# Modulation products of a two-block transformer kernel: column-tile panels replaced by whole-row chunks with quarter products

## The chip, the cores and the metric

One core of a Trainium2 chip runs the whole program in one launch. The metric is the device time in microseconds (us) of one execution; before the change three runs gave 1325.57, 1325.74 and 1326.34 us. The engines are named as in the profile: PE (TensorE matmul), PEld (its weight loads), DVE (VectorE), ACT (ScalarE), POOL (GpSimd) and SP (SyncE, which only issues DMAs here).

## The reference, cut to what matters

Two blocks of two layers each run on 256 tokens of width 1024. The first block is attention, a gated feed-forward and a per-layer embedding, twice. The second block modulates its inputs with vectors made from two conditioning vectors, `c` and `c_ctx`:

```python
mod_x = (silu_c @ w_mod[i] + b_mod[i])[:, None, :]       # silu_c: (1, 1024), w_mod[i]: (1024, 3072)
mod_c = silu_cc @ w_mod[i] + b_mod[i]
sh_x, sc_x, g_x = jnp.split(mod_x, 3, axis=-1)
hx = rms_norm_2(x, norm_g[i]) * (1.0 + sc_x) + sh_x
```

The change touches only the products `silu_c @ w_mod[i]` and `silu_cc @ w_mod[i]`: 1024 rows by 6144 columns over both layers, 25.2 MB of weights, for two vectors. They don't depend on the first block, so the kernel makes them beside it. The first 2048 columns (shift and scale of layer 0) are made during the first attention, 2048 more during each of the two feed-forwards.

## The kernel before, in words

Everything is float32. A large product `x @ w` is made of three fp32r products on PE (lines 417 to 419, `mm3`): high half by high half, high by low, low by high. The weights come as 295 panels of 128 x 1024 (512 KB each). SP loads them into six slots RAW, ACT copies each to its high half WH (line 1848), DVE subtracts to get the low half WL (line 1131), PE uses the pair. Three WH/WL slots turn over. Semaphores alone keep the engines in step; within an engine the order is that of the program text.

**First attention** (`attention("l0", ...)`, line 625). Sixteen units n = 0 to 15, two for each of 8 heads (even n one key block, odd n two). In PE's step n come, in this order: the scores of unit n (line 742), then `fill`, then for odd units the value product of unit n-3 (line 750, in the even steps from 4), then the transposes of unit n-2 (line 651). DVE adds the bias (1359), takes the maximum (1212) and later scales (1187, 1191, 1193). ACT in step n copies the transposes of unit n-2 (1887), makes the exponentials of unit n (1898), and in odd steps from n = 5 copies head (n-5)/2 out of PSUM (1997, `out_l0`), which lets POOL square that head (2523, `head_squares`). After the last unit come two groups of heads: POOL's squares, DVE's sum (1364), ACT's root (2007), DVE's reciprocal (1371) and product (1375), PE's transposes (759, `heads_turn`), ACT's and DVE's halves XH (2013) and XL (1384). Then the output projection `l0_o` begins (line 417, tile G).

**Fillers of the first attention.** `fill` (line 547) makes one 128-column product at a time: stationary the 32 padded vectors SC of k tile k, moving 128 columns of a panel of `w_mod`, plain float32. A panel holds one column tile of 128 columns with its eight k tiles. There are 16 panels and 128 such products: 12 before the attention, 5 in each of its steps 0 to 17, then 14, 6 and 6 around `heads_turn`. Each goes to a strip of 32 partitions of the PSUM bank O; four panels in a row use the same strip. The panels are loaded by POOL's queue (`panels`, line 2494, DMA at 2499) into six slots; before each `head_squares(h)` POOL issues panels up to `6 + (10*h + 35) // 8`: 4 to 9 ahead of the first head, 10 after the first head, and so on.

**Feed-forwards** (`ffn(layer)`). Tiles j = 0 to 21. In a tile PE makes `hidden` (48 matmuls into G, 128 columns of each of two halves), then `down` of the tile two before (24 into A). DVE scales and convolves, ACT and POOL (2473, 2474, 2477: HID, HH, HL) make the gated value that `down` uses. From tile 6 on each tile ends with a `refill` (line 571): a panel of 1024 columns of `w_mod` (two k tiles by 512 columns), which POOL loaded (`gathers`, 2501, DMA at 2509), ACT rounded to fp32r (2081, `high`) and DVE subtracted (1524, `rest`), takes four fp32r products of 512 columns into partitions 0 to 31 of O (line 578). SCR holds the vectors with their low halves (1453 to 1456). Four refills fill 512 output columns; ACT then copies the row to YR. Tiles 19, 20 and 21 and the last two `down` are written out after the loop.

**After each feed-forward**, in `ple`, ACT copies the last row (2139), PE turns the rows to columns (`turn_gathered`, 587), and DVE later adds the parts and the bias (`gathered`, 1413, 1404).

Of the kernel before, what the change touches and what calls it, by code (L numbers as in the profile page):

```python
# [23 lines left out]
P = 128  # L24
# [13 lines left out]
MODS = 48  # L38
PLAIN = 16
GROUPS = 4  # L40
# [95 lines left out]
def program(nc, x_tok, wst, wmod, vec, cst, x_t, ctx_t, p_t, pos, pos4, tab, rpb, lam4, grow, y_t):  # L136
    with ExitStack() as ctx:
# [31 lines left out]
        SCR = sb("SCR", [P, KD, 32], F32R)  # L169
# [51 lines left out]
        RM = mv[:, 6144:12288].rearrange("p (s c) -> p s c", s=RMS)  # L221
# [43 lines left out]
        YR = B[0:32, 2048:4608]  # L265
        RR = RM[:, 0:4, :]
        RH = XH[:, 12:16, :].rearrange("p n t -> p (n t)")
        RL = XL[:, 12:16, :].rearrange("p n t -> p (n t)")
        ROWS = HRS[:, 1, 0:32].rearrange("p (r t) -> p r t", r=2)
# [61 lines left out]
        r_raw = [sem(f"r_raw{i}") for i in range(4)]  # L331
        r_hi, r_lo, r_y = sem("r_hi"), sem("r_lo"), sem("r_y")
# [76 lines left out]
        def _(pe):  # L409
# [154 lines left out]
            def turn_modulators(dst):  # L564

                pe.wait_ge(m_y, 1)
                for q in range(4):
                    m = nc.tensor.transpose(dst[:, q * P:(q + 1) * P], YS[:, q * P:(q + 1) * P], IDT)
                m.then_inc(m_tr, 1)

            def refill(layer, s, i):

                if s == 0:
                    pe.wait_ge(r_y, i + (2 + 5 * layer))
                pe.wait_ge(r_lo, i * 4 + (5 + PLAIN * layer + s))
                for c in range(2):
                    for w in (RH, RL):
                        m = mm(O[0:32, :], SCR[:, 2 * s + c, :], w[:, 512 * c:512 * c + 512],  # L578
                               start=(s == 0 and c == 0 and w is RH), stop=(s == 3 and c == 1 and w is RL),
                               skip_group_check=True)  # L580
                m.then_inc(m_used, 1)

            def turn_gathered(layer):

                pe.wait_ge(r_y, 1 + 5 * (layer + 1))
                for t in range(PLAIN):
                    m = nc.tensor.transpose(O[:, 32 * t:32 * t + 32], YR[:, 512 + t * P:512 + (t + 1) * P], IDT[0:32, 0:32])
                m.then_inc(m_tr, 1)
# [36 lines left out]
            def attention(s, scores, value, filler=0, behind=None, meanwhile=(0, 0), first=0, last=None, ready=()):  # L625
                units = attn_units(s)
                width = 1 if s == "l0" else 2
                for n in range(first, len(units) + 3 if last is None else last):
# [7 lines left out]
                    if n < len(units) + 2:  # L636
                        fill(filler)
# [138 lines left out]
            turn_modulators(A[0])  # L776

            def ffn(layer):
# [37 lines left out]
                def tile(j, i=0, filled=None):  # L816
# [4 lines left out]
                    if filled is not None:  # L821
                        refill(layer, filled, i)

# [1912 lines left out]
```

## Time and profile before

| what | us |
|---|---|
| three timed runs, median | 1325.74 |
| three timed runs, lowest and highest | 1325.57, 1326.34 |
| span of the profiled execution, first to last instruction | 1325.0 |
| PE busy in it | 1271.4 (96%) |
| DVE busy | 945.7 (71%) |
| ACT busy | 723.9 (55%) |
| POOL busy | 391.0 (30%) |

The span is that of one other execution, and the table gives no time of its own for it beyond the span; the timed runs are 0.7 us longer than the span at their median, which is what lies around the first and last instruction. The records of a matmul overlap: its time on the chain is the distance to the next start, not its length. A plain float32 product of this program leaves two records, an fp32r product or a transpose one.

### The profile page before, as it was taken

What the parts mean: (1) busy time and instruction counts of PE and PEld (TensorE: products, weight loads), DVE (VectorE), ACT (ScalarE), POOL (GpSimd) and SP (SyncE); (2) the same over time, 40 slices, a digit from 0 to 9 for tenths busy, and PEclk for the clock granted to TensorE, in tenths of its full rate; (3) what the DMA queues carried; (4) which work ended last, traced back from release to release, by engine and by line L of the source; (5) the groups of instructions that cost most, each with busy time, mean ns of one, the idle gap of its engine ahead of it and who ended that gap; (6) DMA issues with size and microseconds to landing.
All of it is one profiled execution on the core that took longest, in us unless ns stands there. A gap on an engine that the chain in (4) does not pass through costs nothing.

```text
span 1325.0 us, 24391 instructions
## 1 busy us (share of the span) xinstructions
PE 1271.4 (96%) x8908; PEld 1102.8 (83%) x8908; DVE 945.7 (71%) x1426; ACT 723.9 (55%) x1257; POOL 391.0 (30%) x377
## 2 busy tenths in 40 slices
PE   5999999999999999999999999999989999999996
PEld 4887899999999877898999998888855699987666
DVE  6878588888878985558988887853377548454674
ACT  5555455655567777545565657644366515413562
POOL 4942144545431140143445452011012320000022
PEclk9999999999999999999999999999999999999999
DMA  8565246666645542155576663322200274522100
GB/s 309 178 218 191 72 141 233 219 222 219 217 154 172 160 130 96 63 191 171 197 234 211 230 213 128 130 93 95 96 1 1 59 181 133 170 95 80 48 1 32
DMA packets 52665, 191.72 MB, mean 145 GB/s; under 512 B 6048, under 2 KB 6304, under 8 KB 52320
## 3 DMA queue, kind: packets, MB, share of 16 engines
q1 hardware_dynamic: 43488, 158.59, 36.2%
q0 software_dynamic: 8368, 31.33, 7.5%
q8 instruction: 62, 1.02, 0.3%
q10 hardware_dynamic: 720, 0.57, 0.2%
q14 instruction: 27, 0.22, 0.0%
HBM read 189.41 MB, written 1.05 MB: 144 GB/s over the span
## 4 chain that ended last, share of the span: by engine, by line
PE 78%; DVE 9%; ACT 7%; issue 3%; POOL 1%; DMA 1%; SPq 0%; DVEq 0%; ACTq 0%; POOLq 0%
PE G L417 13%; PE G L419 13%; PE G L418 13%; PE A L417 6%; PE A L419 6%; PE A L418 6%; DVE WL L1131 3%; PE R L651 3%; PE R L578 2%; PE R L558 2%; ACT WH L1848 2%; PE A L999 1%; PE R L417 1%; PE R L419 1%; PE R L418 1%
## 5 line engine op out<-in xcount | busy, mean ns | idle before, releaser
L1131 DVE TENSOR_TENSOR WL<-RAW,WH 128x1024 fp32r<-128x1024 f32 x295 | 390.4, 1330 | 245.3 <-ACT WH L1848 244.9
L1848 ACT ACTIVATE WH<-RAW 128x1024 fp32r<-128x1024 f32 x295 | 310.4, 1057 | 387.1 <-PE G L419 275.9
L417 PE MATMUL G<-XH,WH 128*128 128x256 f32 (+1 forms) x1336 | 398.7, 298 | 7.8 <-DVE WL L1131 4.6
L419 PE MATMUL G<-XH,WL 128*128 128x256 f32 (+1 forms) x1336 | 395.4, 296 | 0.0
L418 PE MATMUL G<-XL,WH 128*128 128x256 f32 (+1 forms) x1336 | 395.4, 296 | 0.0
L417 PEld LDWEIGHTS G<-XH,WH 128*128 128x128 f32 x1336 | 255.5, 191 | 21.6 <-issue 10.6
L418 PEld LDWEIGHTS G<-XL,WH 128*128 128x128 f32 x1336 | 255.6, 191 | 7.4
L419 PEld LDWEIGHTS G<-XH,WL 128*128 128x128 f32 x1336 | 255.7, 191 | 6.2
L417 PE MATMUL A<-HH,WH 128*128 128x256 f32 x352 | 99.9, 284 | 1.0 <-POOL HL L2477 1.0
L418 PE MATMUL A<-HL,WH 128*128 128x256 f32 x352 | 99.8, 283 | 0.0
L419 PE MATMUL A<-HH,WL 128*128 128x256 f32 x352 | 99.7, 283 | 0.0
L2453 POOL CAST XH<-HRS 128x256 fp32r<-128x256 f32 x24 | 11.4, 474 | 267.3 <-DVE HRS L1745 267.3
L1212 DVE TENSOR_REDUCE SM<-A 128x2 f32<-128x1024 f32 (+1 forms) x80 | 67.7, 849 | 17.9 <-PE A L999 12.8
L417 PEld LDWEIGHTS A<-HH,WH 128*128 128x128 f32 x352 | 67.6, 192 | 2.2 <-ACT WH L1848 1.9
L1887 ACT ACTIVATE ATT<-R 128x1024 f32<-128x1024 f32 (+3 forms) x56 | 37.7, 674 | 56.8 <-PE R L651 56.8
L418 PEld LDWEIGHTS A<-HL,WH 128*128 128x128 f32 x352 | 67.6, 192 | 0.1
L419 PEld LDWEIGHTS A<-HH,WL 128*128 128x128 f32 x352 | 67.6, 192 | 0.0
L417 PE MATMUL G<-WH,XH 128*128 128x512 f32 (+1 forms) x136 | 54.6, 402 | 12.8 <-DVE XL L1157 11.1
L2473 POOL TENSOR_TENSOR HRS<-ATT,HRS 128x256 f32<-128x256 f32 x22 | 32.0, 1452 | 110.3 <-ACT HRS L2058 104.7
L2473 POOL TENSOR_TENSOR HRS<-HSQ,HRS 128x256 f32<-128x256 f32 x22 | 31.7, 1439 | 98.0 <-ACT HRS L2058 98.0
L417 PE MATMUL A<-WH,XH 128*128 128x512 f32 x144 | 57.4, 398 | 1.5 <-DVE XL L1469 1.3
L419 PE MATMUL A<-WH,XL 128*128 128x512 f32 x144 | 56.2, 390 | 0.0
(355 smaller groups left out, 2532.0 us busy)
## 6 DMA issues: line engine op xcount, KB each, us to landing
RAW<-in_wst SPq DMA_DIRECT2D x295, 512.0 KB, 4.1
M<-in_wmod POOLq DMA_DIRECT2D x48, 512.0 KB, 4.1
B<-in_rpb POOLq DMA_DIRECT2D x4, 1024.0 KB, 12.6
H<-in_x_t SPq DMA_DIRECT2D x2, 512.0 KB, 8.4
M<-in_x_tok SPq DMA_DIRECT2D x1, 1024.0 KB, 13.5
M<-in_ctx_t POOLq DMA_DIRECT2D x1, 1024.0 KB, 5.2
out_y<-M SPq DMA_DIRECT2D x2, 384.0 KB, 2.7
C<-in_cst SPq DMA_DIRECT2D x1, 737.0 KB, 15.1
```

Of the source, the lines that this page charges most:

```text
L417: mm(out, lh, rh, start=start, stop=False, skip_group_check=True)
L418: mm(out, lh, rl, start=False, stop=False, skip_group_check=True)
L419: return mm(out, ll, rh, start=False, stop=stop, skip_group_check=True)
L558: m = mm(out[32 * g:32 * g + 32, q * P:(q + 1) * P], SC[:, k, :], RM[:, i % RMS, k * P:(k + 1) * P], start=(k == 0), stop=(k == KD - 1), s ...
L578: m = mm(O[0:32, :], SCR[:, 2 * s + c, :], w[:, 512 * c:512 * c + 512], start=(s == 0 and c == 0 and w is RH), stop=(s == 3 and c == 1 and ...
L651: m = nc.tensor.transpose(ST[c][:, k * P:(k + 1) * P], PRB[a % 3][:, c, k * P:(k + 1) * P], IDT)
L999: m = mm(out[c][:, 0:nk * P], Q2[64 * c:64 * c + 64, t, qt * P:(qt + 1) * P], K2[64 * c:64 * c + 64, t // 4, k0:512], start=True, stop=Tru ...
L1131: v.tensor_tensor(WL[:, slot, :], RAW[:, raw, :], WH[:, slot, :].bitcast(F32), ALU.subtract).then_inc(w_lo, 1)
L1212: v.tensor_reduce(small(80, a, 2), sc, AX, ALU.max, negate=True).then_inc(at_mx, 1)
L1848: act(WH[:, slot, :], RAW[:, raw, :], ACT.Copy).then_inc(w_hi, 1)
L1887: act(att(s, j)[:, 0:width, 0:nk, q * P:(q + 1) * P], RO[:, :].rearrange("p (l k q) -> p l k q", l=2, k=4)[:, 0:width, 0:nk, :], ACT.Copy) ...
L2473: g.tensor_tensor(HID[b], CB[b][:, 0, :], SG[b], ALU.mult).then_inc(f_hid, 1)
```

## The change: what it does

The weights of the modulation are laid out anew on the host: 24 chunks of 128 x 2048 (1 MB each), one for each k tile and third of the 6144 columns. Everything is plain float32 now; a chunk is made of four products of 512 columns, one for each strip of 32 partitions of O ("quarter products"). In the first attention a chunk is taken in halves, with its two quarter products in one step: two halves ahead of the attention, one in each of the steps 1 to 14, none later. In each feed-forward eight chunks are used whole, one for every second tile, and ACT's and DVE's rounding, the row copies and the low halves SCR go. POOL copies the vectors of the chunk's k tile to SV before it issues each load. The output of a third is one bank O of 128 x 512, which ACT copies to YS and PE turns with four transposes.

```diff
+            def modulate(vectors, buf, start, stop):
+                for g in range(4):
+                    m = mm(O[32 * g:32 * g + 32, :], vectors, RM[:, buf, g, :], start=start, stop=stop, skip_group_check=True)
+                m.then_inc(m_used, 1)
+
             def fill(n):
                 for _ in range(n):
-                    i, k = divmod(fills[0], KD)
-                    if fills[0] == 0:
+                    i = fills[0]
+                    k, half = divmod(i, 2)
+                    if i == 0:
                         pe.wait_ge(m_sil, 1)
-                    if k == 0:
-                        pe.wait_ge(m_raw[i % RMS], 16 * (i // RMS + 1))
-                    g, q = i // 4, i % 4
-                    out = O
-                    m = mm(out[32 * g:32 * g + 32, q * P:(q + 1) * P], SC[:, k, :], RM[:, i % RMS, k * P:(k + 1) * P],
-                           start=(k == 0), stop=(k == KD - 1), skip_group_check=True)
-                    if k == KD - 1:
-                        m.then_inc(m_used, 1)
+                    pe.wait_ge(m_raw[i % RMS], 16 * (i // RMS + 1))
+                    for g in range(2):
+                        r = 32 * (2 * half + g)
+                        m = mm(O[r:r + 32, :], SC[:, k, :], RN[:, i % RMS, 512 * g:512 * g + 512],
+                               start=(k == 0), stop=(k == CHUNKS - 1), skip_group_check=True)
+                    m.then_inc(m_used, 1)
                     fills[0] += 1
...
-                    if n < len(units) + 2:
-                        fill(filler)
+                    if n in filler:
+                        fill(1)
...
-            fill(12)
+            fill(2)
             pe.wait_ge(bias_ok, 1)
-            attention("l0", scores_l0, value_l0, 5)
-            fill(14)
+            attention("l0", scores_l0, value_l0, range(1, 15))
             heads_turn(0)
-            fill(6)
             heads_turn(1)
-            fill(6)
...
                 for j in range(2, 7):
                     tile(j)
+                modulated(0, 0, start=True)
                 with pe.Fori(0, 3) as i:
-                    for d in range(4):
-                        tile(7 + d, i, d)
-                for d in range(3):
-                    tile(19 + d)
-                    refill(layer, d, 3)
+                    tile(7, i)
+                    tile(8, i)
+                    modulated(1, i)
+                    tile(9, i)
+                    tile(10, i)
+                    modulated(0, i + 1)
+                tile(19)
+                tile(20)
+                modulated(1, 3, stop=True)
+                tile(21)
                 down(0, p0 + 64, hb + FT - 1, p0 + 64, False, False)
-                refill(layer, 3, 3)
                 down(1, p0 + 65, hb + FT, p0 + 65, False, True)
...
-                        turn_gathered(layer)
+                        turn_modulators(O, 2 + layer)
...
-                        rest(d, i)
...
-                        high(d, i)
...
-                ac.wait_ge(m_used, PLAIN * (layer + 2))
-                act(YR[:, 2048:2560], O[0:32, :], ACT.Copy).then_inc(r_y, 1)
+                ac.wait_ge(m_used, PLAIN + CHUNKS * (layer + 1))
+                act(YS, O, ACT.Copy).then_inc(m_y, 1)
...
             def panels(first, end):
                 for i in range(first, end):
                     if i >= RMS:
                         gp.wait_ge(m_used, i - RMS + 1)
-                    gp.dma_start(RM[:, i % RMS, :], wmod[i]).then_inc(m_raw[i % RMS], 16)
+                    gp.dma_start(RN[:, i % RMS, :], wmod[i // 2][:, PW * (i % 2):PW * (i % 2) + PW]).then_inc(m_raw[i % RMS], 16)
...
+                g.tensor_copy(SV[:, k % 2, :], vectors).then_inc(r_vec[k % 2], 1)
+                src = wmod[first + k] if k < 2 else wmod[bass.ds(i * 2 + (first + k), 1)].rearrange("a p c -> p (a c)")
+                gp.dma_start(RM[:, k % 2, :, :].rearrange("p g c -> p (g c)"), src).then_inc(r_raw[k % 2], 16)
...
             for h in range(8):
-                upto = min(PLAIN, 6 + (10 * h + 35) // 8)
+                upto = min(PLAIN, 8 + 2 * h)
                 panels(nextp, upto)
                 nextp = upto
                 head_squares(h)
```

## Rows read from the trace of the kernel before

**Rows 1.** The page's busy times: us, share of the span, instructions
```profile
PE 1271.4 (96%) x8908; PEld 1102.8 (83%) x8908; DVE 945.7 (71%) x1426; ACT 723.9 (55%) x1257; POOL 391.0 (30%) x377
```
**Rows 2.** Busy by stretch: us, PE, PEld, DVE, ACT, POOL, PEclk, DMA share, GB/s
```profile
205.80:214.40 8.60, 8.60 (x74) 8.60 (x73) 6.32 (x10) 4.59 (x6) 3.91 (x3) 1.00 0.71 248
240.35:249.89 9.54, 9.54 (x78) 9.13 (x76) 8.18 (x11) 5.43 (x7) 4.50 (x4) 1.00 0.70 241
```
**Rows 3.** Timeline of PE: the starts of two feed-forward tiles without a refill
```profile
205.79 0.28 PE L417 MATMUL G<-XH,WH 128*128 128x256 f32 x1
...
214.44 0.28 PE L417 MATMUL G<-XH,WH 128*128 128x256 f32 x1
```
**Rows 4.** Chain in the first feed-forward: start us, us, what; two refills in a row
```profile
240.52 0.92 PE R L578 x4
...
250.06 0.92 PE R L578 x4
```
**Rows 5.** Timeline of PE, attention of the second block: two column strips of 64
```profile
970.70 1.95 PE L1008 MATMUL G<-ATT,M 128*64 128x256 f32 x16
972.58 1.13 PE L999 MATMUL A<-M 64*128 64x512 f32 x4
```
**Rows 6.** Timeline of the last tile of the first feed-forward
```profile
376.46 1.73 DVE L1524 TENSOR_TENSOR XL<-M,XH 128x1024 fp32r<-128x1024 f32 x1
377.07 1.73 POOL L2474 TENSOR_TENSOR HH<-HSQ,HRS 128x256 fp32r<-128x256 f32 x1
378.94 0.74 POOL L2477 TENSOR_TENSOR HL<-HRS,HH 128x256 fp32r<-128x256 f32 x1
...
379.83 0.36 PE L417 MATMUL A<-HH,WH 128*128 128x256 f32 x1 [0.48 <-POOL HL L2477]
```
**Rows 7.** Timeline of POOL in a tile without `rest`
```profile
217.57 0.75 POOL L2474 TENSOR_TENSOR HH<-ATT,HRS 128x256 fp32r<-128x256 f32 x1
```
**Rows 8.** Timeline of attention step 5, from the transposes to the next load
```profile
110.84 0.44 PE L651 MATMUL R<-C,ATP 128*128 128x128 f32 x2
...
112.49 0.39 ACT L1997 ACTIVATE B<-G 128x256 f32<-128x256 f32 x1
...
112.97 0.61 POOL L2523 TENSOR_TENSOR HRS<-B 128x256 f32<-128x256 f32 x1 [6.05 <-ACT B L1997]
...
113.53 0.59 POOL L2499 DMA_DIRECT2D M<-in_wmod  x1
```
**Rows 9.** Loads of `w_mod`, issued in 98.9:99.3 and in 113.4:114, to landing
```profile
DMA to landing us min/median/max: 6.0/6.0/6.0
DMA to landing us min/median/max: 3.9/3.9/3.9
```
**Rows 10.** Chain in the first attention: the fillers of steps 6 and 14
```profile
111.70 1.21 PE R L558 x10
...
130.54 1.21 PE R L558 x10
```
**Rows 11.** Timeline from the last sum of squares to the output projection
```profile
142.03 1.22 DVE L1364 TENSOR_REDUCE SM<-HRS 128x8 f32<-128x1024 f32 x1 [0.50 <-POOL HRS L2523]
...
144.26 1.26 ACT L2013 ACTIVATE XH<-A,SM 128x512 fp32r<-128x512 f32 x2 [3.44 <-PE A L759]
...
145.42 0.30 ACT L2007 ACTIVATE SM<-SM 128x8 f32<-128x8 f32 x1
...
145.99 1.29 DVE L1375 TENSOR_TENSOR B<-B,SM 128x512 f32<-128x512 f32 x2
...
147.20 2.72 DVE L1384 SCALAR_TENSOR_TENSOR XL<-A,SM,XH 128x512 fp32r<-128x512 f32 x4
...
149.35 0.39 PE L417 MATMUL G<-XH,WH 128*128 128x256 f32 x1
```
**Rows 12.** Timeline of PE: matmuls at the start, and one at 24 us
```profile
12.09 0.63 PE L419 MATMUL G<-WH,XL 128*128 128x512 f32 x1
...
24.30 0.39 PE L419 MATMUL G<-WH,XL 128*128 128x512 f32 x1
```

More of the change, by code:

```diff
@@ L168, in program @@
         SC = sb("SC", [P, KD, 32])
-        SCR = sb("SCR", [P, KD, 32], F32R)
+        SV = sb("SV", [P, 2, 32])
         mv = M[:, :]
@@ L330, in program @@
         sum_step = sem("sum_step")
-        r_raw = [sem(f"r_raw{i}") for i in range(4)]
-        r_hi, r_lo, r_y = sem("r_hi"), sem("r_lo"), sem("r_y")
+        r_raw = [sem(f"r_raw{i}") for i in range(2)]
+        r_vec = [sem(f"r_vec{i}") for i in range(2)]
         h_sq = sem("h_sq")
@@ L567, in turn_modulators @@
                 for q in range(4):
                     m = nc.tensor.transpose(dst[:, q * P:(q + 1) * P], YS[:, q * P:(q + 1) * P], IDT)
[L569 to L587, printed above, removed]
                 m.then_inc(m_tr, 1)
@@ L623, in advance, with attention @@
                     next(unit, None)
-            def attention(s, scores, value, filler=0, behind=None, meanwhile=(0, 0), first=0, last=None, ready=()):
+            def attention(s, scores, value, filler=(), behind=None, meanwhile=(0, 0), first=0, last=None, ready=()):
                 units = attn_units(s)
@@ L815, in ffn, with tile @@
                 hidden(1, p0 + 2, (u0 + 1) % 2, (u0 + 1) // 2, p0 + 2)
-                def tile(j, i=0, filled=None):
+                def tile(j, i=0):
                     q = p0 + 4 + 3 * (j - 2)
@@ L909, in _ @@
                                 + [(1, k) for k in range(8, 16)], T, lambda k: pe.wait_ge(at_g, AJ0["l1"] + k // 2 + 1))
-            attention("l1", scores_l1, value_l1, 0, first_o, (4, 3), first=2, ready=((1, TVALS),))
+            attention("l1", scores_l1, value_l1, (), first_o, (4, 3), first=2, ready=((1, TVALS),))
             advance(first_o, 32)
@@ L1025, in _ @@
             evacuated(pe, U0["a_z"] + 7)
-            attention("a", scores_a, value_a, 0, first_o, (2, 2), first=4)
+            attention("a", scores_a, value_a, (), first_o, (2, 2), first=4)
             advance(first_o, KD)
@@ L1099, in _ @@
             first_o = head_unit("b_o", [(c, k) for c in range(2) for k in range(7)] + [(0, 7), (1, 7)], T, lambda k: pe.wait_ge(at_o, AT_JOBS["a"] + k + 1))
-            attention("b", scores_b, value_b, 0, first_o, (6, 3), first=2, ready=((0, TVALS + 10), (1, TVALS + 12)))
+            attention("b", scores_b, value_b, (), first_o, (6, 3), first=2, ready=((0, TVALS + 10), (1, TVALS + 12)))
             advance(first_o, 2 * KD)
@@ L1397, in with_bias @@
             def with_bias(layer, r, t0, rows):
-                n = rows.shape[-1] if len(rows.shape) == 2 else rows.shape[-1] * rows.shape[-2]
+                n = rows.shape[-1] * rows.shape[-2]
                 at = VC[f"bm{layer}"] + t0
-                dst, bias = MD[:, layer, r, t0:t0 + n], V[:, at:at + n]
-                if len(rows.shape) == 3:
-                    dst, bias = (x.rearrange("p (g q) -> p g q", q=4) for x in (dst, bias))
+                dst, bias = (x.rearrange("p (g q) -> p g q", q=4) for x in (MD[:, layer, r, t0:t0 + n], V[:, at:at + n]))
                 link(v.tensor_tensor(dst, rows, bias, ALU.add))
@@ L1409, in scales, with modulators @@
                                             bc(V[:, VC[f"ng{layer}"]:VC[f"ng{layer}"] + 8], 2), ALU.add, ALU.mult))
[L1411 to L1424 removed]
+            def modulators(made, src, parts):
+                dv.wait_ge(m_tr, made)
+                rows = src.rearrange("p (q g r) -> p r g q", q=4, g=4)
                 for layer, t0, a, b in parts:
                     for r in range(2):
[L1427 to L1430 removed]
+                        with_bias(layer, r, t0, rows[:, r, a:b, :])
+                if made != 2:
+                    scales(made // 2)
+                v.memset(SM[:, 34 + made:35 + made], 0.0).then_inc(m_ok, 1)
             def add_out(tag, per, gain, late):
@@ L2075, in lands @@
                     return [16 * ((p + 3 + d) // RAWS + 1) for d in range(3)]
-                def high(s, i):
-                    ac.wait_ge(r_raw[s], i * 16 + (64 * layer + 16))
-                    ac.wait_ge(m_used, i * 4 + (PLAIN * (layer + 1) + s))
-                    act(RH, RR[:, s, :], ACT.Copy).then_inc(r_hi, 1)
-                def row(i, used):
-                    ac.wait_ge(m_used, used)
-                    act(YR[:, bass.ds(i * 512, 512)], O[0:32, :], ACT.Copy).then_inc(r_y, 1)
                 for j in range(2, 6):
```

76 lines of the change are left out of this document (23 added, 53 removed).

## The prediction

> **What bounds the kernel now.** I read the busy times first, then the chain of waits, then the timeline where the change cuts in. PE is busy for 96% of the span and the next engine for 71% [rows 1], so time is won by taking work from PE, where PE is the engine that nobody has to wait for. The feed-forwards are such a place. A tile without a refill takes 214.44 - 205.79 = 8.65 us [rows 3], a tile with one 250.06 - 240.52 = 9.54 us [rows 4]: the refill's 0.9 us lie bare on the path. In both kinds PE is busy to the last hundredth, while DVE has 6.3 of 8.6 and 8.2 of 9.5 us of work, ACT and POOL less [rows 2]. So the refill's PE time counts in full, and DVE's `rest` and ACT's `high`, which the change also takes out, count for nothing inside the tiles. The first attention is another kind of place: PE, DVE, ACT and POOL hand each unit on, and a pair of steps takes (130.54 - 111.70) / 4 = 4.71 us, of which the two fillers are 2 x 1.21 us [rows 10]. There the order in which POOL issues the loads matters, and that order is changed too.
>
> **Price of a quarter product.** Ten filler records of 128 columns take 1.21 us [rows 10], about 0.11 us each and 0.1 us for going in and out of the narrow strip. A pass over 512 columns is then 4 x 0.107 = 0.43 us, and a plain float32 product has two. Four strips one after the other would be 8 x 0.43 = 3.4 us. But the value products at line 1008, which go in turn to two strips of 64, put 16 passes of 256 columns, 3.4 us if done singly, into 972.58 - 970.70 = 1.88 us [rows 5]: two strips stream at once, at a cost of 0.15 us over half the single time. A half chunk of the attention has two strips: 0.86 + 0.15 = 1.0 us. No row shows four strips. The upper bound is 3.5 us a chunk (none side by side), the next 1.7 + 0.15 = 1.85 us (two by two), the lower 0.86 us (all four with nothing for the change of shape). I take 1.0 us, all four and the 0.15 us, since the nearest row shows different strips of one bank running wholly side by side.
>
> The Trainium skill speaks to this on two pages. *TensorEngine Tiling (Array Packing)*, "Tiling Modes", gives 128 x 32 as four tiles that work independently, and says that a change of mode drains the array; the 0.15 us in [rows 5] agree with the drain. *TensorE: Matmul & The Clock Gate*, "Why this matters for your kernels", reports only 2.38 times for three strips. An estimate by that page, 2.38 / 3 of four, is 3.4 / 3.17 = 1.08 us a chunk, and the sum below would be 1.3 us higher, 1324.5 us.
>
> **Feed-forwards.** In each one 14 refills stand before the last `hidden` ends; they go: 14 x 0.90 = 12.6 us. The last two stand behind it, where PE waits for the gated value of the last tile anyway (its `down` starts at 379.83 on POOL's HL, with 0.48 us of idle PE even behind the refill [rows 6]), so taking them out gives nothing by itself. But that wait gets shorter: POOL's HH took 1.73 us there beside DVE's `rest` [rows 6], and 0.75 us in a tile where no `rest` ran [rows 7]; without it the last `down` starts 1.0 us earlier (bounds 0 and 1.0). Eight chunks come in at 1.0 us. Per feed-forward -12.6 - 1.0 + 8.0 = -5.6 us, for two -11.2 us. The loads are the same bytes, in 1 MB instead of 512 KB; a chunk is issued two tiles (17 us) ahead, and the slowest of the 512 KB loads shown here takes 6.0 us [rows 9], 12 us if doubled, so none is late. POOL's copy of the vectors is below the 0.74 us of HL, which is eight times wider, and POOL is busy for less than half of a tile [rows 2, 6]. If that cover failed, a copy would cost at most 16 x 0.74 = 12 us, and I take 0.
>
> **First attention.** Fill i (from 0) now needs panel i whole, and it stands at step n = i - 1 with i = 2 to 15. POOL issues panels 4 to 7 before the first head's squares, but 8 and 9 only behind them, 10 and 11 behind the second head's, and so on. The first head is copied out by ACT in step 5, at 112.49; POOL squares it at 112.97 and issues the next load at 113.53 [rows 8]; it lands 3.9 us later [rows 9], at 117.4. PE wants panel 8 in step 7, half a pair behind the filler of step 6 at 111.70 [rows 10], at about 114. Before, this load was a panel used only six steps later. So PE stands for some 3.4 us in step 7, in `fill`, with its transposes behind it; ACT waits for those before its exponentials and before it copies the second head out; POOL waits for that head before it issues panel 10. This closes a loop: fill 1.0, transposes to ACT's copy 112.49 - 110.84 = 1.65, to POOL 0.48, to the issue 0.56 [rows 8], landing 3.9 [rows 9], wake-up 0.1, together 7.7 us for each pair of steps, where the others need about 4.3. Panels 10, 12 and 14 land at 125.1, 132.8 and 140.5. Then step 13's fill (1.0), transposes and scores (0.8) bring the filler of step 14 to 142.3 instead of 130.54 [rows 10], +11.8 us. The shorter fillers don't help ahead of this: panel 4 is issued at 99.06 and lands 6.0 us later [rows 9], and its fill, now in step 3 instead of 4, waits for it at 105.1. Behind step 14, DVE's chain of scaling sets the pace, and the filler is 0.2 us shorter: +11.5 us is left for the last unit.
>
> Then the fillers around `heads_turn` are gone. Before, ACT waited 3.44 us for transposes that stood behind 28 filler records, so its root for the second group came at 145.42, although DVE's sum had ended at 143.25 [rows 11]. Now that sum starts at 142.03 + 11.5 = 153.5 and ends at 154.7, ACT's root follows at 154.8, the product 0.57 us behind, the XL halves 1.21 us behind that, two of the four (1.36 us) are needed, and the output projection starts at 158.0 instead of 149.35 [rows 11]: +8.6 us. The 12 fillers ahead of the attention become two half chunks and cost nothing either way, since PE waits there for DVE's bias. Bounds: without any wait on loads this part would be -8 us (rival 3); with a landing of 6.0 us [rows 9] in each loop it would be 4 x 2.1 = 8.4 us worse.
>
> **The rest**: SCR's four small DVE instructions go ahead of a reciprocal that waits for ACT anyway (0). In `ple` ACT's copy of O is 128 partitions deep, and PE turns it with fewer transposes ahead of a gate unit that waits for DVE's weights: +0.1 us together, bounds -1 and +0.5.
>
> **Sum.** The profiled span of 1325.0 us becomes 1325.0 + 8.6 - 11.2 + 0.1 = 1322.5 us; the median of the runs lies 0.7 us above the span: 1323.2 us.
>
> **The rivals.**
> 1. *The strips stream two at a time* (slower). Place: every chunk in the feed-forwards, where [rows 2] leave no idle PE to hide it. Price 1.85 instead of 1.0 us, 16 times: +13.6, 1336.8 us. It decides from 1.16 us a chunk on, where 16 x 0.16 eats the 2.5 us of gain. For it: the only row has two strips [rows 5]. Against: those two run without hindering each other. With none side by side, 16 x 2.5 more: 1363 us.
> 2. *The clock falls in the attention.* PE stands 3.4 us in each of four pairs and waits again in the tail. At the start, after 11 us of rest, a 512-column product shows 0.63 us, at 24 us 0.39 [rows 12]: the difference is one of the two levels, 1.2 and 2.4 GHz. At 1.2 GHz a loop has 1.0 us more for the fill and 0.3 for transposes, and the tail about 1 us: 4 x 1.3 + 1 = +6, 1329 us. The skill's page on TensorE, the same section, warns that idle stretches between bursts put the clock back; that is this rival. Against: PE works for over half of each loop.
> 3. *The loads don't hold the attention up.* Then steps take 4.1 to 4.3 us a pair, the last unit comes 5.2 us earlier and the tail gains 2.9: -8.1 instead of +8.6, 1306.5 us. Against is the order of POOL's program, with ACT as releaser in [rows 8].
> 4. *The 1 MB loads crowd the weight stream*, so that tiles of the feed-forward wait. The DMA share there is 0.70 [rows 2]; a wait of 0.3 us in each of the 16 chunks gives +5, 1328 us.
>
> **How the numbers follow.** Forecast 0.60, strips in twos 0.12, singly 0.03, clock 0.10, no hold-up 0.08, crowding 0.07. The forecast's own range is 1320 to 1327 us (a chunk from 0.9 to 1.15 us, the loop 0.3 us either way). I leave out the 0.08 below and the 0.03 above with the edges: 1319.5 to 1338 us. A difference under 0.2%, 2.65 us, can't be told from none here; the forecast lies near that edge. Faster: half of 0.60, and 0.08: 0.37. Same: the other half, and part of clock and crowding: 0.36. Slower: 0.27.
>
> **What would show it.** A chunk's eight records should fill about 1.0 us of the chain, and a pair of tiles 18.3 us. In the attention, PE should wait for DMA at the fillers of steps 7, 9, 11 and 13, about 3.3 us each, and POOL's loads should be 7.7 us apart; the output projection should start near 158. The last `down` of each feed-forward should start 7.8 us behind the last `hidden`. The prediction is wrong if a chunk is 1.2 us or more, or if PE doesn't stand in step 7.

## The result: 1333.69 us, 0.54% slower, where 1323.2 us was forecast

| | before | after |
|---|---|---|
| median of the timed runs, us | 1326.04 (4 runs, 1325.57 to 1327.01) | 1333.69 (4 runs, 1331.91 to 1334.74) |
| ratio after / before, 95% interval | | 1.0054 (1.0040 to 1.0069) |
| span of the profiled execution, us | 1325.0 | 1332.8 |
| mean granted clock of PE, share of 2.4 GHz | 0.998 | 0.987 |

The time lies in the range of the forecast, but on the other side of no change. To see where it went, I take the start of the same DVE instruction in both traces, at five places: the bias of the first attention, the first weight half behind the start of the output projection, and one place behind each feed-forward and ahead of the second. Here they are in the timeline, DVE alone (start, duration, then what; "x2" merges two instructions). Before:

```profile
93.42 0.68 DVE L1293 TENSOR_TENSOR B<-A,C 128x512 f32<-128x512 f32 x1
156.56 1.23 DVE L1131 TENSOR_TENSOR WL<-RAW,WH 128x1024 fp32r<-128x1024 f32 x1 [1.65 <-ACT WH L1848]
399.57 0.69 DVE L1166 TENSOR_TENSOR ATP<-G,RST 128x512 f32<-128x512 f32 x1
611.62 0.88 DVE L1498 SCALAR_TENSOR_TENSOR ATT<-ATT,V 128x256 f32<-128x256 f32 x2
841.78 0.69 DVE L1561 TENSOR_TENSOR H<-H,ATP 128x512 f32<-128x512 f32 x1
```

After:

```profile
92.36 0.68 DVE L1282 TENSOR_TENSOR B<-A,C 128x512 f32<-128x512 f32 x1
172.34 1.23 DVE L1120 TENSOR_TENSOR WL<-RAW,WH 128x1024 fp32r<-128x1024 f32 x1 [1.92 <-ACT WH L1814]
411.20 0.69 DVE L1155 TENSOR_TENSOR ATP<-G,RST 128x512 f32<-128x512 f32 x1
623.47 0.88 DVE L1470 SCALAR_TENSOR_TENSOR ATT<-ATT,V 128x256 f32<-128x256 f32 x2
849.48 0.69 DVE L1527 TENSOR_TENSOR H<-H,ATP 128x512 f32<-128x512 f32 x1
```

| stage, up to | forecast | measured |
|---|---|---|
| start, 93.42 / 92.36 | 0 | -1.06 |
| first attention, 156.56 / 172.34 | +8.6 | +16.84 |
| feed-forward 0, 399.57 / 411.20 | -5.6 | -4.15 |
| second layer's attention, 611.62 / 623.47 | about +0.1 | +0.22 |
| feed-forward 1, 841.78 / 849.48 | -5.6 | -4.15 |
| rest of the span | 0 | +0.1 |
| sum | -2.5 | +7.8 |

The start can't be put down to the change: over the twelve kernels below, whose code is all but the same there, it ranges from -1.15 to +0.72 us against this one trace of before. Two terms are off, the attention by 8.2 us and each feed-forward by 1.45 us.

**The first attention.** The waits of PE from 90 to 165 us (in all, times, longest):

```profile
PE R L560 <- DMA M<-in_wmod: 13.0, 5, 3.7
PE R L633 <- DVE ATP L1182: 2.5, 1, 2.5
PE A L741 <- DVE B L1364: 2.0, 1, 2.0
```

Five half chunks wait for their load: that of panel 4 in step 3 and those of panels 8, 10, 12 and 14 in steps 7, 9, 11 and 13. It is the closed loop that the forecast described. The chain of waits of the changed kernel, in order of time (start, length, what):

```profile
111.86 0.56 POOL HRS L2476
112.42 4.07 DMA M<-in_wmod
116.53 1.20 PE R L560 x4
117.73 0.64 PE R L633 x2
118.67 1.01 ACT RSQ L1864 x4
119.68 0.28 ACT B L1963
120.04 0.56 POOL HRS L2476
120.60 4.19 DMA M<-in_wmod
124.83 1.92 PE R L560 x4
...
145.10 1.85 PE R L560 x4
...
162.54 0.55 PE G L413
```

POOL squares a head and only then issues the load that PE already wants; PE's transposes let ACT copy out the next head; POOL squares it. The fills that wait start 116.53, 124.83, 133.71 and 141.83: 8.3, 8.9 and 8.1 us a pair of steps, where 7.7 was forecast. What the forecast gave only 0.10 stands in the same rows: a half chunk took 1.20 us at 116.53 and 1.92 us at 124.83. The stretches of the first attention (PE, PEld, DVE, ACT, POOL busy with their instructions, then the granted clock, the DMA share and GB/s), with three short ones around the first of these waits and two inside the second and the fourth:

```profile
112.00:121.00 9.00, 5.65 (x24) 1.92 (x24) 4.99 (x13) 2.54 (x11) 2.50 (x5) 0.81 0.34 117
121.00:130.00 9.00, 6.67 (x26) 2.22 (x26) 4.22 (x11) 2.54 (x11) 1.65 (x4) 0.67 0.35 117
149.00:163.00 14.00, 7.24 (x37) 5.54 (x36) 11.10 (x20) 8.36 (x23) 2.45 (x4) 0.83 0.00 0
163.00:168.50 5.50, 5.50 (x28) 5.50 (x28) 0.71 (x2) 0.46 (x2) 0.00 (x0) 0.50 0.01 3
...
112.50:116.50 4.00, 0.68 (x5) 0.28 (x4) 2.77 (x7) 0.97 (x5) 1.03 (x2) 1.00 0.70 236
116.50:118.00 1.50, 1.47 (x6) 0.43 (x6) 0.00 (x0) 0.00 (x0) 0.00 (x0) 0.77 0.18 71
118.00:119.00 1.00, 1.00 (x6) 0.51 (x4) 0.00 (x0) 0.61 (x2) 0.00 (x0) 0.50 0.00 0
...
124.20:124.80 0.60, 0.00 (x0) 0.00 (x0) 0.56 (x2) 0.00 (x0) 0.00 (x0) 0.50 1.05 416
141.30:141.80 0.50, 0.00 (x0) 0.00 (x0) 0.00 (x0) 0.00 (x0) 0.00 (x0) 0.50 1.04 401
```

In the first wait PE had worked 0.68 of 4.0 us, the clock was still granted in full (1.00), and then, with PE back at work, it went to 0.50, which is 1.2 GHz. In the waits that end at 124.83 and 141.83 it was down already while PE still stood. The output projection starts at 162.54 (forecast: near 158) and its first 5.5 us run at 0.50 throughout: a matmul every 0.21 us instead of 0.12. Before the change the same matmuls began at 149.35 [rows 11] at full clock.

**The feed-forwards.** PE in the timeline around one chunk:

```profile
247.27 0.28 PE L414 MATMUL A<-HL,WH 128*128 128x256 f32 x1
247.39 0.28 PE L415 MATMUL A<-HH,WL 128*128 128x256 f32 x1
247.60 1.07 PE L547 MATMUL R<-M,SV 128*32 128x512 f32 x8
248.59 0.38 PE L413 MATMUL G<-XH,WH 128*128 128x256 f32 x1
248.81 0.28 PE L414 MATMUL G<-XL,WH 128*128 128x256 f32 x1
```

From its first record to the next tile's first it is 0.99 us, as forecast. But the last matmul before it holds its place for 0.21 us (247.39 to 247.60) and the first one behind it for 0.22 us, where 0.12 us is usual. From chunk to chunk it is 18.46 us (247.60, then 266.06), two tiles of 8.65 us [rows 3] and 1.16 us.

### The profile page after: what moved, and what is told of

The parts are those of the page before. It is cut to its first block, busy times and chain, and to the rows that moved or that the text cites. A ratio compares the mean times of both kernels' runs of the same rounds, so it can differ in the third digit from the quotient of the medians.

```text
span 1332.8 us, 23786 instructions
## 1 busy us (share of the span) xinstructions
PE 1256.2 (94%) x8692; PEld 1072.4 (80%) x8692; DVE 883.7 (66%) x1388; ACT 689.6 (52%) x1217; POOL 365.2 (27%) x377
## 3 DMA queue, kind: packets, MB, share of 16 engines
HBM read 189.41 MB, written 1.05 MB: 143 GB/s over the span
## 4 chain that ended last, share of the span: by engine, by line
PE 76%; DVE 8%; ACT 7%; issue 3%; DMA 3%; POOL 1%; SPq 0%; DVEq 0%; ACTq 0%; POOLq 0%
PE G L413 14%; PE G L415 13%; PE G L414 13%; PE A L413 6%; PE A L415 6%; PE A L414 6%; PE R L633 3%; DVE WL L1120 3%; ACT WH L1814 2%; DMA M<-in_wmod 2%; PE R L413 1%; PE R L415 1%; PE R L414 1%; PE A L988 1%; PE G L997 1%
## 5 line engine op out<-in xcount | busy, mean ns | idle before, releaser
L1120 DVE TENSOR_TENSOR WL<-RAW,WH 128x1024 fp32r<-128x1024 f32 x295 | 382.7, 1304 | 292.7 <-ACT WH L1814 292.3
```

The lines of the kernel that those rows point to most:

```text
L1120: v.tensor_tensor(WL[:, slot, :], RAW[:, raw, :], WH[:, slot, :].bitcast(F32), ALU.subtract).then_inc(w_lo, 1)
```

## The experiments

The table has, for each kernel, the stages as above, against the same trace of before, and the median of its timed runs (one run for the last three lines). The kernel before took 1325.64 to 1326.66 us beside them.

| kernel | start | attention | ffn 0 | ffn 1 | median, us |
|---|---|---|---|---|---|
| the change | -1.06 | +16.84 | -4.15 | -4.15 | 1333.69 |
| early | -0.69 | -2.28 | -2.66 | -4.14 | 1316.93 |
| ffn_alone | -0.99 | 0.00 | -4.12 | -4.16 | 1318.06 |
| kept_busy | -1.15 | +24.13 | -2.77 | -4.18 | 1342.65 |
| kept_busy_less | -0.13 | +10.28 | -4.16 | -4.16 | 1328.58 |
| tail_busy | +0.72 | +13.01 | -4.14 | -4.16 | 1331.37 |
| spread | +0.18 | -4.59 | -2.67 | -4.17 | 1314.86 |
| last_chunk | -1.03 | 0.00 | -5.28 | -5.30 | 1315.66 |
| pairs | -0.94 | 0.00 | -6.27 | -6.27 | 1314.23 |
| both | -1.01 | -5.07 | -6.27 | -6.28 | 1308.81 |
| chunk_twice | -0.06 | +13.62 | +2.68 | +2.66 | 1345.74 |
| two_strips | +0.69 | 0.00 | +2.59 | +2.57 | 1332.63 |
| one_strip | -1.12 | 0.00 | +17.46 | +17.81 | 1361.00 |

### early: POOL's loads ahead of its squares

```diff
-                upto = min(PLAIN, 8 + 2 * h)
+                upto = min(PLAIN, 12 + 2 * h)
```

> The changed kernel with one line of POOL's program changed: ahead of head h's squares it issues the loads up to panel 12 + 2h instead of 8 + 2h, so that panel i is issued as soon as its slot is free, some six steps ahead of its half chunk. My theory (POOL's order makes the loads late, PE then stands, and standing drops its clock): no wait for the loads is left in the first attention, its half chunks take 1.0 us each and not 1.8 us, the output projection starts near 145 us instead of 162.5 us, and the kernel takes 1309 us (1306 to 1314). Rival A (the loads are late because the queues are full, whoever issues them when): the waits stay, 1325 to 1334 us. Rival B (the loads alone aren't it; without products in the tail the clock falls there anyway, and the projection runs at half clock at first): 1313 to 1318 us.

Measured: 1316.93 us, ratio to before 0.9926 (0.9913 to 0.9940). One line takes back 19 us of the attention, so the order of POOL's program made the loads late; rival A is out: the loads that PE waited for had landed 4.07 and 4.19 us after their issue, now the loads take 6.4 us (median), side by side, and only one of them is waited for. The wait that is left is the one for panel 4, 2.1 us, and the projection starts at 145.0 us. But 1309 us was too low; rival B came true, in its time and in what it names: the clock still falls in the tail, and the projection begins at half clock. What no expectation had: it falls at the end of feed-forward 0 too. First the stretches of the attention, then two at the end of feed-forward 0:

```profile
112.00:130.00 18.00, 18.00 (x106) 8.07 (x105) 16.76 (x43) 10.54 (x46) 4.59 (x8) 1.00 0.38 128
130.00:149.00 19.00, 12.25 (x64) 9.78 (x63) 12.74 (x23) 8.92 (x24) 2.46 (x4) 0.73 0.00 1
...
372.60:373.40 0.80, 0.73 (x6) 0.76 (x7) 0.80 (x1) 0.00 (x0) 0.00 (x0) 1.00 0.72 287
373.40:376.80 3.40, 3.40 (x18) 3.40 (x18) 0.21 (x1) 0.00 (x0) 0.00 (x0) 0.51 0.46 161
```

PE had stood for 1.84 us ahead of 372.67, waiting for POOL's last HL; 0.8 us after it had resumed, its clock was at 1.2 GHz for 3.4 us, at a cost of 1.5 us (-2.66 instead of -4.15).

### ffn_alone: the feed-forwards' part of the change by itself

```diff
-            fill(2)
+            fill(12)
...
-            attention("l0", scores_l0, value_l0, range(1, 15))
+            attention("l0", scores_l0, value_l0, 5)
+            fill(14)
             heads_turn(0)
+            fill(6)
             heads_turn(1)
+            fill(6)
...
-                upto = min(PLAIN, 8 + 2 * h)
+                upto = min(PLAIN, 6 + (10 * h + 35) // 8)
```

`fill` and the layout of the first 2048 columns are as before too.

> The first attention as before (160 fillers of 128 columns, the fillers around the turns of the heads, POOL's old order of loads), with the chunks of quarter products in both feed-forwards. My theory: each feed-forward gains 4.2 us as the trace of the changed kernel shows (14 refills of 0.90 and 1.0 us in the tail gone, eight chunks at 1.17 us in), and nothing else moves: 1326.0 - 8.4 = 1317.6 us, or 1316.5 us if the 1.1 us that the changed kernel gains in the first 35 us comes with it. Rival (the feed-forwards gain only because they start later and find their weights staged further ahead): 1321 us or more.

Measured: 1318.06 us, 0.9936 (0.9922 to 0.9950). The two parts add up: the feed-forwards give 8.3 us with the old attention as with the new one, unless the clock falls behind them (below).

### kept_busy and kept_busy_less: the waits stay, the standing goes

```diff
+            def idle(n):
+                for _ in range(n):
+                    m = mm(O[0:32, :], SV[:, 0, :], C[:, 0:512], start=False, stop=False, skip_group_check=True)
+                return m
...
+                    if i in (4, 8, 10, 12, 14):
+                        idle(2 if i == 4 else 3)
                     pe.wait_ge(m_raw[i % RMS], 16 * (i // RMS + 1))
...
+                            if s == "l0" and n == len(units) + 1:
+                                idle(2)
                             pe.wait_ge(at_p, a + 1)
...
             heads_turn(0)
+            idle(2)
             heads_turn(1)
+            idle(1).then_inc(m_used, 1)
```

This is kept_busy_less (`idle` multiplies by a vector of zeros); kept_busy has `idle(6)` ahead of the five half chunks, 4 and 4 at the first two places of the tail and 4 more ahead of `heads_turn(0)`.

> The changed kernel, and while PE waits in the first attention it multiplies by a vector of zeros into the same bank: six products of 512 columns (about 2.6 us at full clock) ahead of the half chunks of panels 4, 8, 10, 12 and 14, four ahead of the last unit's transposes, four ahead of each turn of the heads. Loads and their order stay. My theory (part of the loss is the lower clock, part the wait): the granted clock stays at 2.4 GHz, half chunks take 1.0 us and not 1.8 us, the waits for the loads all but vanish into the extra products, pairs of steps take 7.7 us, the projection starts near 158 us as predicted and without 2.6 us of half clock: 1325 us (1323.5 to 1328). Rival (the clock is a bystander; the loads' order sets all of it): no gain, 1333 to 1336 us.

Measured: 1342.65 us, 1.0119 (1.0104 to 1.0135), slower than the change. The clock stayed up (1.00 all through the first attention), but I had the price of a product wrong: two passes of 0.43 us, 0.87 us each, so that six filled 5.2 us. It tells only that I had mis-sized it, hence:

> As kept_busy, with the products by zero cut to what the waits hold. There each took 0.87 us and six stood in each wait: 5.2 us instead of the 3.3 us of the wait. Now two ahead of panel 4's half chunk, three (2.6 us) ahead of those of panels 8, 10, 12 and 14, two ahead of the last unit's transposes, two between the turns of the heads and one behind them. Theory (the wait alone is the +8.6 of the prediction, the rest is the lower clock): the clock stays at 2.4 GHz, pairs of steps in the loop take about 7.7 us, half chunks 1.0 us, the projection starts near 157 us and runs at full clock from its first product; 1325.5 us (1323.5 to 1328). Rival (the clock costs nothing that the waits on the loads don't take anyway): 1332 us or more.

Measured: 1328.58 us (11 runs, 1326.67 to 1331.17), 1.0016 (1.0007 to 1.0025): 5.1 us less than the change, although PE does 19 x 0.87 = 16.5 us more work. The half chunks in the timeline, POOL's row of it between them, and two stretches:

```profile
117.59 1.05 PE L569 MATMUL R<-M,SC 128*32 128x512 f32 x4 [0.65 <-DMA M<-in_wmod]
119.36 1.05 PE L569 MATMUL R<-M,SC 128*32 128x512 f32 x4
125.70 1.05 PE L569 MATMUL R<-M,SC 128*32 128x512 f32 x4 [0.98 <-DMA M<-in_wmod]
...
120.70 0.76 POOL L2491 TENSOR_TENSOR HRS<-B 128x256 f32<-128x256 f32 x1 [6.09 <-ACT B L1978]
121.41 1.12 POOL L2465 DMA_DIRECT2D M<-in_wmod  x2
...
112.00:130.00 18.00, 16.36 (x77) 6.06 (x73) 10.73 (x26) 6.40 (x30) 4.70 (x8) 1.00 0.35 118
130.00:149.00 19.00, 16.18 (x74) 6.17 (x73) 11.10 (x26) 7.35 (x33) 2.47 (x5) 1.00 0.34 111
```

The clock is 1.00 everywhere, a half chunk takes 1.05 us, and the loop still 8.1 us (117.59 to 125.70): 0.65 to 0.98 us of each wait is left over, so the added products don't set it. The attention costs 10.28 us: the waits for the loads, less the fillers that went. The 6.6 us up to 16.84 are the clock, in this one execution of the change. In another execution of the same attention, that of chunk_twice, it costs 13.62 us, and the clock 3.3 us; the medians of the runs differ by 5.1 us. The time is 0.6 us above the range of the theory, since the loop takes 8.1 us instead of 7.7, and the clock is not up in every run: the eleven runs have mean clocks from 0.994 (1331.17 us, the slowest) to 0.998.

### tail_busy: the same in the tail alone

Against kept_busy_less:

```diff
-                    if i in (4, 8, 10, 12, 14):
-                        idle(2 if i == 4 else 3)
```

> The changed kernel with the products by zero of kept_busy_less in the tail of the first attention alone (two ahead of the last unit's transposes, two between the turns of the heads, one behind them); nothing in the waits for the loads. kept_busy_less, with both, came to 1328.6 us against 1333.7 us. Theory (the clock falls anew at each place where PE stands, so each place is paid for by itself): the output projection no longer starts with 2.6 us at 1.2 GHz, but half chunks in the loop still take 1.8 us: 1331 us (1330 to 1332.5). Rival 1 (the tail is all of it): 1328 to 1329.5 us. Rival 2 (once down in the loop, the clock stays down whatever PE does in the tail): 1333 to 1335 us.

Measured: 1331.37 us, 1.0040 (1.0026 to 1.0054), in the range of the theory; the attention costs 13.01 us. The clock was 1.00 in the projection's start (163.00 to 168.50) but 0.91 and 0.82 in the loop (112 to 130 and 130 to 149 us), and 0.88 in the tail (149 to 163 us). Taking 13.01 from 16.84 doesn't price the tail, because the loop's clock differs between the executions: 0.74 and 0.80 in the change in the same two stretches. The traces give the split themselves. The table has the time between four landmarks: DVE's bias as above, its last scaling (the last unit), the first matmul of the projection, and the weight half as above.

| us | bias to last scaling | to the projection | to the weight half |
|---|---|---|---|
| kept_busy_less | 56.40 | 9.82 | 7.20 |
| the change | 60.28 | 9.90 | 9.80 |
| tail_busy | 58.42 | 10.52 | 7.21 |

Of the change's 6.6 us, 3.9 were paid up to the last unit, 0.1 in the tail behind it and 2.6 in the projection. tail_busy gets back the 2.6; the rest of its gain, 1.9 us up to the last unit, is a clock that fell less in that execution, ahead of where its products stand.

### chunk_twice, two_strips, one_strip: what a chunk is made of

```diff
                 for g in range(4):
-                    m = mm(O[32 * g:32 * g + 32, :], vectors, RM[:, buf, g, :], start=start, stop=stop, skip_group_check=True)
+                    r = 32 * (g % 2)
+                    m = mm(O[r:r + 32, :], vectors, RM[:, buf, g, :], start=start, stop=stop, skip_group_check=True)
```

This is two_strips; in one_strip `r` is 0. In chunk_twice a loop `for n in range(2)` stands around the four products, to four strips.

> The changed kernel with every chunk of the feed-forwards issued twice (16 records instead of eight; the modulation comes out doubled). Theory: four strips stream side by side at 0.43 us a pass, and the rest of the 1.19 us that a chunk costs is going in and out of the narrow shape, once per chunk: the doubled chunk costs 0.87 us more, 16 x 0.87 = 13.9 us, 1347.6 us. Rival (each product costs its share of 1.19 us, whatever its neighbours): 16 x 1.19 = 19 us, 1352.7 us. With strips two at a time the second chunk would cost 1.7 us: 1361 us.

> ffn_alone, with the four products of a chunk of the feed-forwards going to two strips in turn (0, 1, 0, 1) instead of four: the same work for PE, sums in the wrong place. Theory (each strip takes 0.43 us a pass, different strips of the bank stream at once): the chunk's passes take 4 x 0.43 = 1.73 us instead of 0.87 us, 16 x 0.87 = 13.9 us above ffn_alone (1318.1): 1332 us. Rival (with orders in turn a strip isn't free at once, all are in a row): as one_strip.

> ffn_alone, with all four products of a chunk going to strip 0. Theory: eight passes in a row, 8 x 0.43 = 3.5 us and 0.3 us for in and out, 2.6 us more a chunk than with four strips: 1318.1 + 16 x 2.6 = 1359.7 us. Rival (passes to one strip overlap as well, and the number of records sets the price): below 1350 us.

Measured: 1345.74, 1332.63 and 1361.00 us, where 1347.6, 1332 and 1359.7 were expected; each theory holds. The 1.9 us that chunk_twice lies below are less than the 3.2 us that its first attention took less than the change's, and in one_strip the clock fell behind both feed-forwards. The chunk in the timeline of the three, with the record behind it; first chunk_twice:

```profile
245.37 1.92 PE L548 MATMUL R<-M,SV 128*32 128x512 f32 x16
247.22 0.39 PE L413 MATMUL G<-XH,WH 128*128 128x256 f32 x1
```

Then two_strips:

```profile
251.82 1.91 PE L548 MATMUL R<-M,SV 128*32 128x512 f32 x8
253.66 0.39 PE L413 MATMUL G<-XH,WH 128*128 128x256 f32 x1
```

And one_strip:

```profile
251.71 3.62 PE L548 MATMUL R<-M,SV 128*32 128x512 f32 x8
255.26 0.39 PE L413 MATMUL G<-XH,WH 128*128 128x256 f32 x1
```

Up to the next record it is 3.55 us with one strip, 1.84 us with two, 0.99 us with four, and 1.85 us for twice the work in four. The passes take 0.43 us each and different strips hide each other wholly, up to all four; the second set of a doubled chunk cost 0.86 us (feed-forward 0: 2.68 + 4.15 = 6.8 us over eight chunks). What stays is 1.16 - 0.86 = 0.3 us for each time that PE goes into the narrow shape and out again.

### spread: half chunks where PE stands

```diff
-            attention("l0", scores_l0, value_l0, range(1, 15))
+            attention("l0", scores_l0, value_l0, (1, 2, 4, 5, 6, 7, 8, 9, 10, 11, 12, 17))
+            fill(1)
             heads_turn(0)
+            fill(1)
             heads_turn(1)
```

> As early, with the half chunks at other steps: steps 1, 2, 4 to 12, 17, one ahead of each turn of the heads; none in step 3, where the run early still waited 2.1 us for panel 4, and three in the tail, where PE stood for 0.6 to 2.5 us at a time and its clock fell. Theory: the wait of 2.1 us goes, and the tail's clock stays high more of the time, at 1.0 us where the 1.2 GHz level cost 2.6 us in the projection: 1312 us (1309 to 1314), with a smaller spread from run to run. Rival (a half chunk in the tail delays the transposes that ACT and DVE wait for, as the 28 fillers did before): 1316 to 1318 us.

Measured: 1314.86 us (1312.42 to 1316.36), 0.9908 (0.9894 to 0.9921). That is 0.9 us above the range of the theory. Against early the attention gains 2.3 us, in three parts by the landmarks above: 2.1 us up to the last scaling (42.02 against 39.92 us behind the bias), which is the wait for panel 4; 1.2 us lost from there to the projection (10.26 against 11.44), where the three half chunks now stand; and 1.4 us gained in the projection, which runs at full clock here (8.58 against 7.18). So the rival's delay and the theory's gain are both there. The clock still fell: 0.82 from 130 to 149 us, and feed-forward 0 lost its 1.5 us again. The spread between runs, 3.9 us, goes with the clock: the two fastest runs (1312.42 and 1312.94 us) have mean clocks of 0.996 and 0.994, the other three 0.992.

### last_chunk and pairs

```diff
-                modulated(1, 3, stop=True)
                 tile(21)
+                modulated(1, 3, stop=True)
...
                     tile(8, i)
-                    modulated(1, i)
                     tile(9, i)
                     tile(10, i)
+                    modulated(1, i)
                     modulated(0, i + 1)
```

Both stand on the kernel of ffn_alone. The first hunk alone is last_chunk; in pairs POOL also issues the loads in the order in which chunks are used.

> As ffn_alone, with the last chunk of each feed-forward moved behind the last `hidden`, where PE stands for 1.9 us until POOL's last HL. Theory: the chunk's 1.17 us lie in that wait: 2 x 1.17 = 2.3 us less than ffn_alone, 1315.7 us, and the projection behind it can't fall to the lower clock, as it did for 3.4 us in the run early. Rival (the last `down` waits for something else by then, or the chunk's loads are late there): 1317.5 to 1318.5 us.

> As last_chunk, with chunks 1 and 2, 3 and 4, 5 and 6 side by side, one pair every four tiles, instead of one chunk every two. Theory (from chunk_twice: 0.87 us for a chunk's passes, 0.3 us for going in and out of the narrow shape): three changes of shape fewer in each feed-forward, 6 x 0.3 = 1.8 us less than last_chunk, 1313.9 us. Rival (the 0.3 us is a gap that the weight stream needs anyway, or two chunks at once leave POOL's or DVE's work late): as last_chunk or slower.

Measured: 1315.66 us, 0.9917 (0.9904 to 0.9931), and 1314.23 us, 0.9911 (0.9896 to 0.9926). Against ffn_alone each feed-forward gains 1.15 us, the chunk's price, and PE's wait for the last HL shrinks from 1.9 to 0.7 us, as the waits of last_chunk from 350 to 380 us say:

```profile
PE A L413 <- POOL HL L2432: 0.7, 1, 0.7
```

With three changes of shape fewer each gains 1.0 us more, 0.33 us for each change. The medians of these two lie 1.4 us apart with overlapping intervals; the stages, one trace of each kernel but alike in both feed-forwards, decide it.

### both: the fastest

> The attention of spread with the feed-forwards of pairs. If the gains simply add up: pairs lies 3.8 us under ffn_alone (1318.06 to 1314.23 us), and spread is 1314.9 us with single chunks: 1311.0 us (1309.5 to 1312.5), the fastest here. Rival (the gain in the tail of the feed-forwards is a matter of the clock, which falls there in some runs only, and more often behind an attention in which it fell): 1312.5 to 1314 us, and more spread between runs than in pairs.

Measured: 1308.81 us (1307.18 to 1310.07), 0.9869 (0.9854 to 0.9884): 17.5 us less than before, 24.9 us less than the change. It came 2.2 us under the sum, and below the expected range. The stages of the profiles put 1.5 us of that into the tail of feed-forward 0, which spread's profile had lost to the clock, and where here the chunk stands in the wait, and 0.5 us into the attention, where the clock was 0.91 from 130 to 149 us and not 0.82.

## Why the prediction was wrong

**The step that failed** is the term "+8.6" of the first attention, by its premise that PE's clock stays at 2.4 GHz ("Against: PE works for over half of each loop"). It measured +16.84, 8.2 us more than forecast: 6.6 us are the clock, and 1.7 us a hold-up by the loads that was sized too small (10.28 us instead of 8.6). Rival 2 named the mechanism and priced it at +6, with which the forecast would have been 1329 us. That 6.6 us came is in part luck: the rival had 5.2 us in the loop and 1 us in the tail, the trace has 3.9 us up to the last unit and 2.7 us behind it, 2.6 of them in the projection, and another execution of the same attention lost 3.3 us in all.

The clock is the largest part of the miss and not the only one: with the clock held up the change still came out 0.16% slower than before (kept_busy_less), where 0.2% faster was forecast, for the loop and for the chunks below. The chance of 0.10 was the error of judgement on the clock: the profile of before shows no stall of 3 us behind warm work, so neither "it falls" nor "it doesn't" had a row, and the rows at the start [rows 12] were only the two levels. That PE works for over half of a loop did not keep the clock up: PE was busy for 5.65 of 9.00 us in a stretch with the clock at 0.81, and in early for 12.25 of 19.00 us at 0.73. The Trainium skill's page *TensorE: Matmul & The Clock Gate*, section "Why this matters for your kernels", which the prediction cited for rival 2, warns of idle stretches between matmul bursts; the changed kernel agrees, with the clock going down in or behind waits of 2.0 to 3.68 us. The page speaks of longer stretches than the 1.84 us behind which the clock fell in early.

**Right, point by point.** PE stood in steps 7, 9, 11 and 13, for 3.35, 2.33, 1.65 and 3.68 us (forecast: about 3.3), and for 1.94 us in step 3, for panel 4. The two short waits lie behind half chunks at half clock: part of the slower work was done in time that PE would have waited. The hold-up without the clock is 10.28 us (kept_busy_less) where 8.6 was forecast: the loop is 8.1 us and not 7.7. In kept_busy_less it is 3.11 us from fill to POOL (117.59 to 120.70; forecast 3.13), 0.71 to the issue (0.56) and 4.29 to the next fill (4.0 with the wake-up): the load and POOL's squares are the 0.4 us, and three further pairs make 1.2 of the 1.7 us. Rival 3 (no hold-up) is what early makes true in its mechanism, but not in its size: -2.28 us in early and -5.07 us in both, where it had -8.1.

**A chunk** was 1.16 us, not 1.0. The streaming was better than forecast, 0.86 us for four strips; the change of shape costs 0.3 us instead of 0.15. I had read the 0.15 (which the rows give as 1.88 - 1.71 = 0.17) from [rows 5], where the narrow products stand among each other, as the whole price, while the matmuls on both sides of a chunk lose 0.1 us each as well. Eight times 0.16 is 1.3 of the 1.45 us that each feed-forward fell short; the rest is rounding, since [rows 3] and [rows 4] give 0.89 us for each of the 14 refills and not 0.90. Rival 1 was wrong (two_strips shows what it would have cost), though 1.16 us is just its turning point of no gain. Rival 4 was wrong: the tiles stay at 8.65 us while the 1 MB loads land in 6.4 us.

**The tail of the feed-forwards** gave the forecast 1.0 us: POOL's HH no longer runs beside `rest` and takes 0.73 us instead of 1.73, and the last `down` starts 7.9 us behind the last `hidden` (8.9 before; forecast 7.8). But "taking them out gives nothing by itself" missed that the last two refills kept PE busy in that wait. Without them PE stands for 1.9 instead of 0.48 us [rows 6], twice in each of ten profiles here, and behind 5 of these 20 waits the clock fell: in feed-forward 0 of early, kept_busy, spread and one_strip, and in feed-forward 1 of one_strip. In the first three it cost 1.4 to 1.5 us.

**The sum again:** -1.1 (start) + 10.3 (loads, less the fillers) + 6.6 (clock) - 8.3 (feed-forwards) + 0.3 = +7.8 us.

One slip of arithmetic: the prediction's own chances give 0.38 for faster, and not 0.37.

What stays open: why the clock fell behind 5 of the 20 waits of 1.9 us and not behind the others, and why the same attention cost 16.84 us in one execution and 13.62 us in another; no run here can control it.

## What to carry to other kernels

When work leaves an engine that was always busy, check two things that its busy share hid: which queue issues the loads of what is left, and behind which instruction (here one line of POOL's order was worth 17 us), and whether the engine now stands long enough to lose its clock. Put the leftover work where the engine must wait anyway: the same chunk costs 1.16 us between two tiles and nothing in the wait ahead of the last `down`. Narrow products are cheap side by side, in as many strips as there are, and dear to enter: group them.

## What the runs showed of the hardware

- Plain float32 products of 512 columns into different 32-partition strips of one PSUM bank run side by side: 3.55 us with one strip, 1.84 us with two, 0.99 us with four. The steps of 1.71 and 0.85 us are four and two passes of 0.43 us, so that two passes are seen where eight run. The Trainium skill's page *TensorE: Matmul & The Clock Gate*, section "Why this matters for your kernels", has 2.38 times for three strips; the estimate by it, 1.08 us a chunk, was nearer to the 1.16 us than mine, but these rows put the loss into the change of shape and not into the streaming.
- Where PE's clock falls is not fixed by the wait. In the changed kernel it was granted 1.00 in a wait (112.5 to 116.5 us) and 0.50 from 118 us on, with PE back at work; in two later waits it was 0.50 while PE still stood (124.2 to 124.8 and 141.3 to 141.8 us). In early it fell 0.8 us after the end of a wait of 1.84 us. Behind 15 of 20 such waits (1.84 to 1.86 us, ahead of the last `down`) it did not fall at all.
- Products by zero that PE makes while it would wait keep the clock up: 1.00 from 112 to 149 us in kept_busy_less, against 0.74 and 0.80 in the change, and 5.1 us less in all, with 16.5 us of added work.
- The kernel before, with no wait of PE above 1.4 us behind its first 24 us, repeats within 1.4 to 2.0 us (three sets of 9, 15 and 9 runs, all of them from 1325.32 to 1327.46); with waits of 2 us and more the runs of one kernel lie up to 5.3 us apart (early, 5 runs: 1313.57 to 1318.82), while ffn_alone, whose longest waits are two of 1.85 us, keeps within 1.5 us (5 runs: 1316.87 to 1318.37).
